# First layer's down projection in twin tiles, five double chunks of each twin by seven block products

## The reference

```
x = x + (silu(xn @ w_gate) * (xn @ w_up)) @ w_down      # w_gate, w_up: 2048 x 5632, w_down: 5632 x 2048
```

## Time and profile before

| what | us |
|---|---|
| median of three runs (2084.47 to 2087.18) | 2086.71 |
| the profiled execution, its own time | 2080.63 |
| its span, first to last instruction | 2078.8 |
| TensorE busy | 2068.8 |
| VectorE busy | 1600.6 |
| ScalarE busy | 1097.3 |
| first layer's down, 794.18 to 1033.54 | 239.36 |
| second layer's down, 1842.01 to 2075.16 | 233.15 |

### The profile page before, as it was taken

One profiled execution on the slowest core, in us unless ns is written; L12 is line 12 of the kernel. 1 busy time (PEld: TensorE's weight loads), 2 busy tenths in 40 slices (PEclk: granted clock), 3 DMA queues, 4 the chain that ended last, 5 costly groups with the idle time before them and its releaser, 6 DMA issues.

```text
span 2078.8 us, 26999 instructions
## 1 busy us (share of the span) xinstructions
PE 2068.8 (100%) x9168; PEld 1709.3 (82%) x9168; DVE 1600.6 (77%) x2157; ACT 1097.3 (53%) x1424; POOL 76.4 (4%) x85
## 2 busy tenths in 40 slices
PE   9999999999999999999999999999999999999999
PEld 7888888788888888888888888888888888888887
DVE  5777668788888886665576777597888888888887
ACT  6555555555555554444455566555555555555453
POOL 0100011000000000000011000010000000000000
PEclk9999999999999999999999999999999999999999
DMA  8788666667677776656677774667767677766664
GB/s 275 223 269 253 210 207 203 212 213 232 204 239 225 223 221 216 198 187 205 195 233 238 236 225 153 202 194 224 216 214 224 202 245 219 233 221 200 221 200 158
DMA packets 250989, 450.54 MB, mean 217 GB/s; under 512 B 17808, under 2 KB 50704, under 8 KB 250896
## 3 DMA queue, kind: packets, MB, share of 16 engines
q1 hardware_dynamic: 248448, 445.15, 68.3%
q10 hardware_dynamic: 2448, 4.21, 0.6%
HBM read 421.76 MB, written 27.53 MB: 216 GB/s over the span
## 4 chain that ended last, share of the span: by engine, by line
PE 91%; DVE 3%; DMA 3%; issue 1%; ACT 1%; SPq 0%; POOL 0%; DVEq 0%; ACTq 0%
PE psum L902 17%; PE psum L904 17%; PE psum L903 17%; PE psum L777 12%; PE psum L780 12%; PE psum L778 12%; PE psum L831 1%; PE psum L845 1%; DVE w_lo L1418 1%; DMA w_raw<-in_ab_w_in 1%; DMA w_raw<-in_w_up 1%; DMA w_raw<-in_w_down 1%; DMA block_dram<-turn_sb 1%; PE psum L797 0%; ACT w_hi L1019 0%
## 5 line engine op out<-in xcount | busy, mean ns | idle before, releaser
L1019 ACT ACTIVATE w_hi<-w_raw 128x1024 fp32r<-128x1024 f32 (+1 forms) x700 | 732.0, 1050 | 812.5 <-PE psum L904 362.0
L1418 DVE TENSOR_TENSOR w_lo<-w_raw,w_hi 128x1024 fp32r<-128x1024 f32 (+1 forms) x700 | 835.0, 1207 | 349.1 <-ACT w_hi L1019 342.5
L902 PE MATMUL psum<-w_hi,xt_hi 128*128 128x512 f32 x1168 | 454.6, 389 | 0.0
L903 PE MATMUL psum<-w_lo,xt_hi 128*128 128x512 f32 x1168 | 454.5, 389 | 0.0
L904 PE MATMUL psum<-w_hi,xt_lo 128*128 128x512 f32 x1168 | 454.5, 389 | 0.0
L902 PEld LDWEIGHTS psum<-w_hi,xt_hi 128*128 128x128 f32 x1168 | 219.2, 188 | 45.7 <-DVE w_lo L1418 0.2
L903 PEld LDWEIGHTS psum<-w_lo,xt_hi 128*128 128x128 f32 x1168 | 219.2, 188 | 45.6
L904 PEld LDWEIGHTS psum<-w_hi,xt_lo 128*128 128x128 f32 x1168 | 219.3, 188 | 45.4
L777 PE MATMUL psum<-w_hi,xt_hi 128*128 128x512 f32 x604 | 243.2, 403 | 0.8 <-ACT stages L1215 0.8
L777 PE MATMUL psum<-w_hi,ht_hi 128*128 128x512 f32 x608 | 240.7, 396 | 0.0
L780 PE MATMUL psum<-w_hi,ht_lo 128*128 128x512 f32 x608 | 236.9, 390 | 0.0
(11 more groups left out here) (217 smaller groups left out, 2187.0 us busy)
## 6 DMA issues: line engine op xcount, KB each, us to landing
w_raw<-in_w_gate SPq DMA_DIRECT2D x176, 512.0 KB, 4.5
w_raw<-in_w_up SPq DMA_DIRECT2D x176, 512.0 KB, 4.4
w_raw<-in_w_down SPq DMA_DIRECT2D x168, 512.0 KB, 4.7
w_raw<-in_cd_w_in SPq DMA_DIRECT2D x80, 512.0 KB, 4.2
w_raw<-in_ab_w_in SPq DMA_DIRECT2D x71, 512.0 KB, 4.9
block_dram<-turn_sb SPq DMA_DIRECT2D x40, 512.0 KB, 4.9
w_raw<-in_ab_w_out SPq DMA_DIRECT2D x32, 512.0 KB, 4.6
w_raw<-in_cd_w_out SPq DMA_DIRECT2D x32, 512.0 KB, 3.9
```

What stands on the lines that cost most here:

```text
L902: nc.tensor.matmul(acc, a_hi, b_hi, start=start, stop=False)
L903: nc.tensor.matmul(acc, a_hi, b_lo, start=False, stop=False)
L1019: nc.scalar.activation(w_hi[:, slot, 0:n, :], w_raw[:, slot, 0:n, :], ACT.Copy).then_inc(hi_ready, 1)
L1418: nc.vector.tensor_tensor(w_lo[:, slot, 0:n, :], w_raw[:, slot, 0:n, :], w_hi[:, slot, 0:n, :].bitcast(F32), ALU.subtract).then_inc(lo_rea ...
```

## The change

The first layer's down projection gets the form of the second's. `SEVEN`, `TWIN_UNITS`, `PLAIN_END`, `TWIN_END` and `SEVEN_END` get an entry for each layer; helper counts get a layer. Core of the diff:

```diff
-DOWN_UNITS = [(k, 2) for k in range(0, 20, 2)] + [(k, 1) for k in range(20, 24)] + [(k, 2) for k in range(24, HC, 2)]
-SEVEN = ((6, 9, 12, 15, 18), (3, 6, 9, 12, 15, 18))
-PLAIN_END = 19
+SEVEN = (((3, 6, 9, 12, 15), (3, 6, 9, 12, 15)), ((6, 9, 12, 15, 18), (3, 6, 9, 12, 15, 18)))
+PLAIN_END = (16, 19)
...
+        low_t_hi, low_t_lo = (t[:, KC - 8:KC, :].rearrange("p c t -> p (c t)").rearrange("p (k n) -> p k n", k=4)
+                              for t in (xt_hi, xt_lo))
+        DOWN_T = ((low_t_raw[:], low_t_hi, low_t_lo), (t_raw[:], t_hi_sb[:], t_lo_sb[:]))
+        DOWN_S = ((up_a_raw, up_s_raw, low_s_hi[:], low_s_lo[:]), (a_raw[:], s_raw[:], s_hi[:], s_lo[:]))
...
 (TensorE, before the first step of seven of a pair of tiles)
+                            elif first and layer == 0:
+                                pe.wait_ge(acc_free[0], TOK * (pd["a"] + 2))
...
 (ScalarE)
-            def twin_tiles():
+            def twin_tiles(layer):
...
+                            if d and layer == 0:
+                                act.wait_ge(ssq_done, 2 + XT * LN_OF["down", 0])
...
+                        if layer == 0 and i == TWIN_END[0][0] + LEAD + 3:
+                            residual_ssq(0, "down", 2 * d)
+                        if layer == 0 and d == 1 and i == 0:
+                            residual_hi(0, "down", 0)
+                        if layer == 0 and d == 1 and i == LEAD + 2:
+                            residual_ssq(0, "down", 1)
+                        if layer == 0 and d == 1 and i == LEAD + 3:
+                            residual_hi(0, "down", 1)
...
+                        if layer == 1 and p == 0 and k == 0:
+                            residual_hi(0, "down", 2)
...
 (VectorE, residual_add)
+                if name == "down":
+                    dve.wait_ge(x_combined, n // 2 + 1)
...
 (VectorE, twin_tiles(layer); order within unit i)
                         if d == 0:
-                            finish_last(1, i)
+                            finish_last(layer, i)
+                        if layer == 0 and d == 1 and i == LEAD - 1:
+                            residual_add(0, "down", 1)
+                        if layer == 0 and i == TWIN_END[0][0] + LEAD:
+                            residual_add(0, "down", 2 * d)
+                        u = twin_unit(layer, d, i)
+                        if not seven or j == 0:
                             split(u, i % RING)
+                        if seven and j == 0:
+                            row_lows(down_rows(layer, d, p), s_of, high, low)
+                            sum_lows(down_sum(layer, d, p), DOWN_T[layer])
+                        if seven and j == 1:
                             split_lower(u, i % RING)
+                        if ahead and j == 0:
+                            row_sums(down_rows(layer, d, p + 1), p + 1, (ht_hi, ht_lo), a_of, s_of)
+                        if ahead and j == 1:
+                            weight_sums(u + 1, (i + 1) % RING, down_sum(layer, d, p + 1), DOWN_T[layer])
+                        if i == SEVEN_END[layer] + LEAD:
+                            combine(layer, d)
+                        if layer == 0 and d == 1 and LEAD - 1 <= i < LEAD + 3:
+                            turn(0, "down", 1, i - LEAD + 1)
+                        if layer == 0 and 0 <= i - TWIN_END[0][0] - LEAD < 4:
+                            turn(0, "down", 2 * d, i - TWIN_END[0][0] - LEAD)
+                        if layer == 0 and d == 1 and i == 1:
+                            residual_lo(0, "down", 0)
+                        if layer == 0 and d == 1 and i == LEAD + 4:
+                            residual_lo(0, "down", 1)
...
 (VectorE, second layer's input projection)
+                        if layer == 1 and p == 0 and k == 1:
+                            residual_lo(0, "down", 2)
```

More of the change, by code:

```diff
@@ L285, in encoder @@
         w_lo = sb("w_lo", [P, RING, UC, N], F32R)
-        stages = sb("stages", [P, 4, TOK, N])
+        with ExitStack() as whole:
+            stages = sb("stages", [P, 4, TOK, N], c=whole)
+        sb("stage0_pad", [P, TOK, N])
+        low_s_hi = sb("low_s_hi", [P, 4, P], F32R)
+        low_s_lo = sb("low_s_lo", [P, 4, P], F32R)
+        sb("stage23_pad", [P, 2, TOK, N])
         stage = [stages[:, k] for k in range(4)]
@@ L733, in _ @@
                     up_tile(i, UP_KINDS[i - 1], UP_KINDS[i - 2])
[L734 to L752, removed]
+                for d in range(XT // 2):
+                    for i, (j, p) in enumerate(TWIN_UNITS[layer]):
+                        n = 2 * d + j
+                        if d == 0:
+                            move_hidden(layer, HT - 1, i, TENTH)
+                            move_hidden(layer, HT - 2, UPU + i, NINTH)
+                        load(twin_unit(layer, d, i), i % RING, w_down[layer], UC * p, UC, slice(n * N, n * N + N))
         @block.tensor
@@ L1099, in rows_hi @@
                 nc.scalar.activation(high, raw, ACT.Copy).then_inc(s_hi_ready, 1)
-            def twin_tiles():
+            def twin_tiles(layer):
+                _, raw, high, _ = DOWN_S[layer]
                 for d in range(XT // 2):
-                    for i, (j, p) in enumerate(TWIN_UNITS):
-                        u = twin_unit(d, i)
-                        if p in SEVEN[d] and j == 1:
+                    for i, (j, p) in enumerate(TWIN_UNITS[layer]):
+                        u = twin_unit(layer, d, i)
+                        seven = p in SEVEN[layer][d]
+                        if seven and j == 1:
                             split_lower(u, i % RING)
@@ L1387, in _ @@
                 up_tile(layer, UP_LAST, False, True, NINTH, TWIN)
[L1389 to L1406 removed]
+                twin_tiles(layer)
             act.wait_ge(stored, 16 * TOK * (XT + 1))
@@ L1922, in twin_tiles @@
                 for d in range(XT // 2):
-                    for i, (j, p) in enumerate(TWIN_UNITS):
+                    for i, (j, p) in enumerate(TWIN_UNITS[layer]):
+                        seven, ahead = p in SEVEN[layer][d], p + 1 in SEVEN[layer][d]
                         if d == 0:
-                            finish_last(1, i)
-                        if d == 1 and i == LEAD - 1:
+                            finish_last(layer, i)
+                        if layer == 1 and d == 1 and i == LEAD - 1:
```

213 lines of the change are left out of this document (86 added, 127 removed).

## The result

| | us |
|---|---|
| changed kernel, median of four runs (2098.49 to 2101.89) | 2100.61 |
| kernel before on the same chip, median of four (2084.47 to 2087.18) | 2085.63 |
| ratio, 95% interval | 1.0081 [1.0067, 1.0095] |
| two later measurements of the changed kernel beside the one before | 1.0059 [1.0042, 1.0076] and 1.0060 [1.0045, 1.0076] |

The account below looks back on a forecast made before the run. TensorE, busy for the whole span, was taken as the bound. -6.8 + 4.4 + 9.1 + 1.2 = +7.9 us made 2088.5 of the profiled 2080.63, or 2094.6 for the timed runs; range 2083 to 2101.

Parts of the forecast that it names:

- The matmuls, -6.8: First layer's down projection: ten steps of 21 matmuls for 24 save 30 matmuls at 0.2267 us, -6.8 us.
- VectorE's load: First layer's down projection: VectorE busy for 213.5 us in about 233, or 92%; with the waits, a stage of about 246.
- The second pair's start, 7.0: Units 5 to 7 of the second pair: turns of finished tiles make splits late, waits 1.8, 3.0 and 2.2 us.
- The first pair, 4.4: First pair of tiles: TensorE waits 0.3, 2.2, 1.5 and twice 0.2 us at the five steps, 4.4 in sum.
- The second pair's later steps, 2.1 (1.7 + 0.4): Second pair after its first step: 1.7 us lost at the next step, 0.4 at three more.
- Into the second layer, 1.2: Second layer's input projection, unit 6: lateness of 2.7 us less 1.4 of slack loses 1.2 us, bounds 0 and 3.
- The clock, "I add nothing for it": TensorE's clock behind waits: a 1.20 us wait left it at 1.00, so no time was added for a lower level.
- Rival 1: Whole kernel: TensorE stays the bound, waits only 1.1 us, -5.7 us, time 2081.0; chance 0.13.
- Rival 2: Lateness half as large: waits at the same places but 7 us in all, no change, 2087; chance 0.22.
- Rival 3: Loads in bursts take 8 us, each of ten steps costs about 1.4 more: +8 to +20, 2104; chance 0.12.

Follow-up runs that it names:

- e7_early: Changed kernel with seven steps (21 matmuls fewer than before), even tiles ending earlier, turns, parts and last hidden tile's moves shifted; 2077.12 us against 2078.32 before, ratio 0.9994.
- e2: Changed kernel without the second pair's first step of seven (its steps at pairs 6, 9, 12, 15); 2085.74 us against 2077.20 before, ratio 1.0039.
- e5: Changed kernel with the residual work of tiles 0 and 1 spread further apart over the second pair; 2082.88 us against 2078.32 before, ratio 1.0019.
- e8_after: The changed kernel again, unaltered, on a second chip; 2090.25 us against 2078.32 before, ratio 1.0059.
- e14_after: The changed kernel again, unaltered, on a third chip; 2091.15 us against 2078.24 before, ratio 1.0060.
- first trace: Profiled execution of the changed kernel from its first measurement, span 2096.7 us; median of the timed runs 2100.61 us.
- e1_entry: Changed kernel, but the second layer's first unit waits for tile 2's residual add, not tile 3's; 2086.87 us against 2077.20 before, ratio 1.0050.
- e3: Changed kernel with one step of seven in each pair of tiles in place of five; 2082.61 us against 2077.20 before, ratio 1.0024.
- e4: Changed kernel with the last hidden tile's moves at unit 22 instead of 20, low part at 24; 2091.36 us against 2077.20 before, ratio 1.0062.

## Why the prediction was right in direction and wrong in size

The profiled execution's span grew by 17.9 us for the 7.9 of the sum. Of the 10.0 too many, 2.0 are waits in these two stages (16.7 for 14.7), 4.7 the lower clock and small delays of matmuls, 3.9 the second layer's down, and -0.6 the rest. The direction and the places of the waits were right. Two terms were wrong by more than noise: the wait at the entry to the second layer, and the clock.

**The matmuls, -6.8**: right; 30 are gone, and e7_early shows 21 paid out in its two stages, where nothing waits.

**VectorE's load**: predicted 213.5 us busy, 215.2 measured; that is 85% of the longer stage and not over 90%. The stage was put at about 246 without its end; without the 2.86 there it is 249.4, 245.3 and 248.0 in the three traces.

**The second pair's start, 7.0**: right, 6.6 measured in each of them, and place by place: 1.8, 3.0, 2.2 predicted, 1.71, 2.96, 1.9 found. TensorE's unit 0 starts 1.71 plus five units of 2.72 before 931.24, at T = 915.9. The layout had split(5) end at T + 15.4 = 931.3 and it ends at 931.2; split(6) at 937.0, found 936.9; the last split at 940.6, found 940.4. e2 and e5 remove the wait, the one by taking away the step, the other by moving the turns and parts. Where VectorE had no idle time, its order could be laid out by hand to 0.2 us.

**The first pair, 4.4**: 4.61, 3.27 and 3.70. The second step was right (2.2, found 1.93). The third was put at 1.5, which fits e8_after and e14_after (1.48 and 1.78), and measured 2.7 in the first trace (0.75 + 1.93): its load came 4.75 us after VectorE was free, and not the 3.1 that the earlier trace rows show for the same place in the second layer. Unit 8 and the last two steps, put at 0.3 and 0.4, lost nothing.

**The second pair's later steps, 2.1 (1.7 + 0.4)**: 2.63, near nothing, 3.04. The mean, 1.9, is near the forecast, but with a spread of 3 us over three traces that is partly luck.

**Into the second layer, 1.2: a step that failed.** The prediction carried the lateness to unit 6 of the input projection, because it asked when TensorE wants the low part of the turned tile. That lateness is real: e1_entry shows 1.2 us of it. It did not ask what TensorE's first matmul there waits for: the counter of freed accumulators, which the last tile's residual add raises. The banks themselves are free (tile 3 has 6 and 7, the first unit 0 and 1); it is the kernel's bookkeeping that holds TensorE. Its own working had the time: residual_lo ends "at T + 2.0", and the add follows. With T = 1042.41 that is 1044.4, and the row stands at 1044.43. Within the stage nobody is kept waiting by this (the next pair of tiles begins in other banks), so it was computed as VectorE's queue and not as a wait. Before, the add's first half was at 1032.48, ahead of T. The cost is 2.85 or 2.86 us in all three traces and in e2, e3 and e4, instead of 1.2; e1 takes it away by dropping the counter, e7, among several changes, by making the turned tile's low part before the stage ends.

**The clock, "I add nothing for it": the larger failure.** The evidence was one wait of 1.20 us, and the change makes waits of up to 2.96. The granted clock behind two of them was 0.50 and 0.51, for some 3 us each, which cost 3.0 us in the first trace. e8_after lost 3.7 in the same way, also behind two waits, and e14_after, with waits of like length, nothing. The Trainium skill (TensorE: Matmul & The Clock Gate, HAM oscillation) describes throughput lost to falls of the clock and recovery between bursts of matmuls. The first trace and e8_after agree with it; e14_after and e5_spread, whose wait of 3.52 left the clock at 1.00, show that not every gap brings it. The prediction gave it no price; by these traces it is 0 to 4 us.

**Left over.** In the first trace 3.9 us stand in the second layer's down, which the change doesn't touch; e8_after has 0.5 there and e14_after 1.9. Its waits are at the last splits of steps, as in the earlier trace rows, only longer (0.54 to 1.00, five of them), and the median landing time of that stage's own loads was 5.4, 5.1 and 5.4 us in the three traces, 4.9 before. Why loads of a stage 800 us later land later is not shown.

**The rivals.** Rival 1 (TensorE stays the bound) is refuted: VectorE at 85% of the stage (215 of 252) was not its limit by the mean, and stopped TensorE eleven times. The Trainium skill (Perfetto Trace Analysis, Identifying the Most-Contended Engine) was read too simply in the prediction: it calls the busy share of matmuls a poor measure for TensorE and takes that of the weight loads instead. By that measure TensorE had 83% before (198.20 of 239.36) against VectorE's 60%, and now has 76% (192.74 of 252.29) against VectorE's 85%, so the page names VectorE, and the trace agrees. No share says where a wait falls, though: the one at the stage's end is the same 2.69 us with VectorE at 68% and at 85%. Rival 2 (waits of 7 us in all) had less than half of the 16.7 that came. Rival 3 (loads in bursts) has its mechanism at the steps, but in the first trace it makes up only 1.7 us of the excess in this stage (1.2 at the third step, 0.5 at the second pair's later ones), and in e8_after the later steps wait less than forecast; it asked for 8 to 20.

## What to carry to other kernels

When an engine at 85% feeds one near 100%, write out the slower one's order by the clock and hold each item against everything that waits for it, counters of freed buffers among them, not only against those that want the data. Then ask whether such a counter guards a buffer that is really shared. Put bulky work that no one waits for (turns, low parts) in units without extra load; the same work cost 6.6 us in one place and 0.8 in another (e5_spread). A saving of matmuls is kept only as far as the feeding engines have slack: seven steps kept 4.6 of 4.8 us of their stage in their best execution, and no gain of the whole kernel clear of noise; ten lost 12 to 15.

## What was not expected of the hardware

- TensorE's granted clock fell to its lower level behind some waits of 1.9 to 2.9 us and stayed there for 6 to 11 matmuls, which then start 0.425 us apart instead of 0.227. Waits of like length in another execution of the same kernel left it at 1.00, and so did the longest of all, 3.52 us in e5_spread.
- Moving the block moves by two units moved the late load on to the next step (e4_move). The same program has waits for loads that differ by 3 us between traces, each on its own chip, while its waits for VectorE's order agree within 0.04.
